# Attention units of a two-layer encoder: transposes and value products in pairs of steps, and the rounding of the outputs on GpSimd

## The reference

```
for l in range(DEPTH):                       # DEPTH = 2
    h = rmsnorm(x, norm_attn[l])
    z = h @ w_in[l]                          # columns are split among the groups
    o_a = gqa_axial_mixer(...)               # A: 8 heads of 64, softmax(q k^T) v
    o_b = mla_mixer(...)                     # B: 4 heads, scores of 96 channels
    o_c = diff_alibi_mixer(...)              # C: 4 heads, p1 - lambda p2
    x = x + concatenate([o_a, o_b, o_c]) @ w_out[l]
    h = rmsnorm(x, norm_ffn[l])
    x = x + conv_gated_mlp(h, ...)
return rmsnorm(x, final_norm)
```

## Time and profile before

| | us |
|---|---|
| median of 3 runs (2949.03 to 2953.87) | 2949.53 |
| the profiled execution, its own time | 2959.07 |
| its span, first to last instruction | 2957.3 |
| PE busy | 2864.6 |
| DVE busy | 1991.4 |
| ACT busy | 1315.0 |
| POOL busy | 460.7 |

### The profile page before, as it was taken

One profiled execution on the slowest core, in us unless ns is written; L12 is line 12 of the kernel. 1 busy time (PEld: TensorE's weight loads), 2 busy tenths in 40 slices (PEclk: granted clock), 3 DMA queues, 4 the chain that ended last, 5 costly groups with the idle time before them and its releaser, 6 DMA issues.

```text
span 2957.3 us, 36854 instructions
## 1 busy us (share of the span) xinstructions
PE 2864.6 (97%) x13552; PEld 2275.1 (77%) x13552; DVE 1991.4 (67%) x2316; ACT 1315.0 (44%) x1844; POOL 460.7 (16%) x243
## 2 busy tenths in 40 slices
PE   7999889999999999999999998899999999999998
PEld 6777646888888888888877785478788888888887
DVE  3987888982465565556678888889716555565555
ACT  4327888993322222222333288889724122222223
POOL 2111332233300000000131123322241000000002
PEclk9999999999999999999999999999999999999999
DMA  5455332431221111111135533244212111112102
GB/s 199 161 163 128 86 83 61 103 104 58 57 59 56 43 43 56 43 43 43 42 134 203 172 92 72 65 88 109 97 46 69 43 58 43 43 43 66 47 29 57
DMA packets 236532, 236.67 MB, mean 80 GB/s; under 512 B 59520, under 2 KB 199680, under 8 KB 236416
## 3 DMA queue, kind: packets, MB, share of 16 engines
q1 hardware_dynamic: 236416, 235.13, 28.1%
HBM read 184.24 MB, written 50.86 MB: 79 GB/s over the span
## 4 chain that ended last, share of the span: by engine, by line
PE 82%; DVE 10%; issue 4%; ACT 3%; DMA 1%; SPq 0%; ACTq 0%; POOL 0%; DVEq 0%
PE ps L1837 31%; PE ps L1852 16%; PE ps L1574 11%; PE ps L1676 9%; PE ps L1551 5%; PE ps L1714 4%; PE ps L1715 3%; DVE ps L1270 2%; PE ps L1817 1%; PE ps L1710 1%; DVE r L1255 1%; PE ps L1605 1%; DVE r L1298 0%; DVE r L1292 0%; DVE ch L1222 0%
## 5 line engine op out<-in xcount | busy, mean ns | idle before, releaser
L1676 PE MATMUL ps<-stack 128*128 128x512 f32 (+1 forms) x1152 | 350.5, 423 | 45.5 <-ACT prob L942 17.9
L1468 DVE TENSOR_TENSOR xT<-ps,xT 128x512 f32<-128x512 f32 x352 | 241.5, 691 | 209.8 <-PE ps L1852 209.5
L1676 PEld LDWEIGHTS ps<-stack 128*128 128x128 f32 (+1 forms) x1152 | 209.7, 194 | 160.1 <-ACT prob L942 51.5
L1551 PEld LDWEIGHTS ps<-ident_r,prob_r 128*128 128x128 f32 x2048 | 233.2, 143 | 101.3 <-issue 23.9
L942 ACT ACTIVATE prob<-ps,nmx 128x1024 f32<-128x1024 f32 x256 | 285.2, 1114 | 20.9 <-PE ps L1551 10.7
L1433 DVE SCALAR_TENSOR_TENSOR cv<-u,vec,cv 128x1024 f32<-128x1024 f32 x176 | 225.8, 1283 | 89.0 <-ACT cv L1083 78.7
L1378 DVE TENSOR_TENSOR ptl<-ps,pth 128x512 fp32r<-128x512 f32 x384 | 256.5, 685 | 38.6 <-ACT pth L1004 34.8
L1095 ACT ACTIVATE ah<-cv 128x1024 fp32r<-128x1024 f32 x44 | 46.7, 1061 | 528.9 <-DVE cv L1446 528.9
L1837 PE MATMUL ps<-xgh,w0h 128*128 128x512 f32 x704 | 274.7, 390 | 0.0
L1837 PE MATMUL ps<-xgl,w0h 128*128 128x512 f32 x704 | 273.9, 389 | 0.0
L1837 PE MATMUL ps<-xgh,w0l 128*128 128x512 f32 x704 | 273.9, 389 | 0.0
(11 more groups left out here) (245 smaller groups left out, 5555.6 us busy)
## 6 DMA issues: line engine op xcount, KB each, us to landing
wraw<-in_w_up SPq DMA_DIRECT2D x88, 512.0 KB, 5.0
draw<-in_w_down SPq DMA_DIRECT2D x22, 1024.0 KB, 4.9
stack<-ka_d SPq DMA_DIRECT2D x64, 256.0 KB, 5.6
wraw<-in_w_in SPq DMA_DIRECT2D x30, 512.0 KB, 4.2
vst<-v_d SPq DMA_DIRECT2D x48, 256.0 KB, 3.8
x_d<-xT SPq DMA_DIRECT2D x2, 4096.0 KB, 17.6
wraw<-in_w_out SPq DMA_DIRECT2D x16, 512.0 KB, 5.2
stack<-qc_d SPq DMA_DIRECT2D x64, 128.0 KB, 3.5
```

The source lines that it names most:

```text
L1468: ins = dve.tensor_tensor(xs, ps[:, 4 + j % 4, :], xs, ALU.add)
L1551: return pe.transpose(dst.bitcast(F32R), src, ident_r[:, :])
L1676: ins = pe.matmul(score_banks(i)[:, kh, :], st[q][0:rows, c0:c0 + P], st[k][0:rows, kh * HALF:(kh + 1) * HALF], start=n == 0, stop=n == le ...
```

## The change

A unit is **paired** when it is of A or B, three of its next unit's items are still to be made in it, and the unit after that is not of C. That holds for units 1 to 5 (B) and 16 to 30 (A) of each layer. In a paired unit:

- TensorE runs two steps at a time: a score item, the transposes of both steps, then the value products of both. The items come in steps 0, 2, 4 and 6 (they came in 1, 3, 5 and 7); the spread of the reciprocals comes in step 7 behind the products (it came in step 6).
- VectorE takes the maxima in steps 0, 2, 4 and 6, ahead of the low part.
- ScalarE makes the exponentials by a new table `PAIRED_EXP`: item 0 in step 0 ahead of the high copy, and items 1, 2 and 3 behind the high copies of steps 1, 3 and 5 (they came behind those of steps 0, 2, 4 and 6). `copy_norm` comes in step 7.

For all units of A and B, GpSimd writes the rounded result to `xgh` (a copy of 64 partitions x 512), between its own multiplication and its low part; ScalarE's `hi_mix` does nothing there any more. C is unchanged.

```diff
+        def paired(x, nx, after):
+            return x["group"] != "C" and own_items(nx) == 3 and not (after and after["group"] == "C")
+        PAIRED_EXP = {0: 0, 1: 1, 3: 2, 5: 3}
...
                 def lo_mix(x):
                     rows = slice(HD * x["par"], HD * x["par"] + HD)
+                    if x["group"] != "C":
+                        pool.tensor_copy(mix_at(xgh, x), osum[rows, :]).then_inc(mix_hi, 1)
                     pool.wait_ge(mix_hi, l * NU + x["u"] + 1)
...
                 def hi_mix(x):
+                    if x["group"] != "C":
+                        return
...
                 def act_unit(x, prev, nx, after):
                     for s in range(8):
                         second = nx and nx["group"] == "C"
-                        item = EXP_STEP_OF[own_items(nx)].get(s) if nx else None
-                        if second and item is not None:
+                        pairs = paired(x, nx, after)
+                        item = (PAIRED_EXP if pairs else EXP_STEP_OF[own_items(nx)]).get(s) if nx else None
+                        before_copy = second or pairs and s == 0
+                        if before_copy and item is not None:
                             exp_item(nx, item)
...
-                        if not second and item is not None:
+                        if not before_copy and item is not None:
                             exp_item(nx, item)
                         if s == 3 and prev:
                             copy_part(prev)
                         if s == 7 and prev:
                             hi_mix(prev)
-                        if s == (7 if x["group"] == "C" else 6):
+                        if s == (7 if x["group"] == "C" or pairs else 6):
                             copy_norm(x)
...
-                hi_mix(last)
...
+                        n = s + 1 if pairs else s
+                        if nx and n in STEP_OF[own_items(nx)]:
+                            max_item(nx, STEP_OF[own_items(nx)][n])
+                        if pairs:
+                            if s == 6 and after:
+                                max_item(after, 0)
...
+                        if pairs and s % 2 == 0:
+                            if s + 1 in STEP_OF[own_items(nx)]:
+                                score_item(nx, STEP_OF[own_items(nx)][s + 1])
+                            elif after:
+                                score_item(after, 0)
...
-                        if s >= LAG:
-                            value_product(x, s - LAG)
-                        elif prev:
-                            value_product(prev, 8 + s - LAG)
-                        if s == 6:
+                        if not pairs:
+                            products(s)
+                        elif s % 2:
+                            products(s - 1)
+                            products(s)
+                        if s == (7 if pairs else 6):
                             pe.wait_ge(dinv_done, l * NU + x["u"] + 1)
```

More of the change, by code:

```diff
@@ L1369, in dve_unit @@
                             mix_maps(nx, MIX_STEPS[s])
-                        if nx and s in STEP_OF[own_items(nx)]:
-                            max_item(nx, STEP_OF[own_items(nx)][s])
-                        if after and s in EARLY_STEP_OF[after["group"]]:
+                        pairs = paired(x, nx, after)
+                        n = s + 1 if pairs else s
[4 more added lines that the diff above has]
+                                max_item(after, 0)
+                        elif after and s in EARLY_STEP_OF[after["group"]]:
                             max_item(after, EARLY_STEP_OF[after["group"]][s])
@@ L1732, in pe_unit, with products @@
                 def pe_unit(x, prev, nx, after):
-                    b = x["half"]
-                    for s in range(8):
-                        if nx and s in STEP_OF[own_items(nx)]:
+                    b, pairs = x["half"], paired(x, nx, after)
+                    def products(n):
+                        if n >= LAG:
+                            value_product(x, n - LAG)
+                        elif prev:
+                            value_product(prev, 8 + n - LAG)
+                    for s in range(8):
+                        if pairs and s % 2 == 0:
[3 more added lines that the diff above has]
+                                score_item(after, 0)
+                        elif not pairs and nx and s in STEP_OF[own_items(nx)]:
                             score_item(nx, STEP_OF[own_items(nx)][s])
-                        if after and s in EARLY_STEP_OF[after["group"]]:
+                        if after and not pairs and s in EARLY_STEP_OF[after["group"]]:
                             score_item(after, EARLY_STEP_OF[after["group"]][s])
```

## The result

The changed kernel takes 2999.75 us (median of 4 runs, 2996.58 to 3005.87) against 2950.95 us before (4 runs): ratio 1.0162, 95% interval 1.0148 to 1.0176. Forecast were 2988.0 us, 2956 to 3010, slower with 0.88. Its profiled execution took 2998.46 us.

What follows compares the result with a forecast made beforehand. PE, busy 97%, was taken as the bound, with VectorE and ScalarE nearly full in A. Per layer 15 x 1.15 + 5 x 0.4 = 19.3 us, 38.5 for two, on the median 2949.53 gave 2988.0 us, range 2956 to 3010.

Steps and rivals of the forecast that it cites:

- The signs: Profile marks listed beforehand: longer periods, VectorE idle ahead of `sum_output`, PE idle ahead of step 6's transposes, PE below 92% in A.
- PE's own work: Per pair, transposes lose 0.05 us and the second value product gains 0.07: net gain 0.02, 3 us over 40 paired units.
- The new wait in A: Per paired unit, late `copy_part` holds VectorE, then PE at steps 6 and 7: 1.40 us, net +1.15 on 10.89.
- 1.6 if all small waits stay: Upper end given for the +1.15 us per paired unit of A; it entered the range's top as 30 x 1.6.
- B, 0.4 us: Per paired unit of B, the same chain with longer items: PE waits 0.50 us, less 0.08, so +0.4 us.
- I cost the relief at nothing: ScalarE losing 24 rounding copies of 0.626 us per layer: nothing gained, at most 0.4 us per unit of A.
- GpSimd's copy: The 64 x 512 rounding copy on GpSimd: taken as 1.29 us, hidden behind GpSimd's idle time.
- The first: Rival: the wait never forms if `copy_part` is done at about 2.4 us; 15 us faster, 2934 us; chance 0.09.
- the main case: The full wait forms in paired units, `copy_part` ending at 3.24 us after step 3's start: 2974 to 3004 us, chance 0.68.
- The second, half the wait: Rival: step 6 stalls but VectorE recovers, or `copy_part` starts sooner; +0.2 to +0.8 us per A unit, 2956 to 2974; chance 0.12.
- The third, a falling clock: Rival: PE's clock falls as well, one to four falls worth 5 us each over both layers, 2993 to 3008 us; chance 0.08.

Runs made afterwards that it cites:

- e3: The changed kernel with `copy_part` directly behind the high copy of step 3, ahead of the exponential, in paired units: 2969.59 us, ratio 1.0054 to the kernel before.
- e4: The changed kernel with `sum_output` two steps later (step 5 instead of 3) in paired units: 2962.45 us, ratio 1.0028 to the kernel before.
- e8: No unit paired, GpSimd rounds, `copy_part` in step 4 behind the exponential in units of A and B: 3043.42 us, ratio 1.0306 to the kernel before.
- e7: e4 with the value product lagging two steps instead of three, in every unit: 2947.52 us, ratio 0.9982 to the kernel before.
- e9: The changed kernel with no unit paired, GpSimd still rounding, value product lagging two steps instead of three: 2946.09 us, ratio 0.9980 to the kernel before.
- e2: The changed kernel with the rounding back on ScalarE for every unit, so the pairs alone: 3013.64 us, ratio 1.0204 to the kernel before.

## Why the prediction was right

It was right in direction, range and mechanism. The median lies 11.8 us above the number, and by the periods the difference can be placed: 8 us in A, 3 in B, and 1 in the median of the kernel before, which stood that much higher here. The signs came as listed: VectorE idle 1.0 us ahead of `sum_output` (0.7 to 1.0 forecast), PE idle 1.24 us ahead of step 6's transposes (1.1), PE 90% busy in A (below 92%), and no wait of GpSimd for ScalarE in A's units. e3 and e4 took the wait away in two ways and most of the loss went with it; e8 made it without pairs.

- **PE's own work, 0.02 us saved per pair.** Right in its parts, not confirmed as a gain. In the timeline above eight transposes take 571.95 - 571.32 = 0.63 us, and a product behind a product starts after 0.23 (572.25 to 572.48 in the same timeline). But only 24 of the 49 runs of eight in 500 to 650 us take 0.63 to 0.65; 11 take 0.71 to 0.75 and 14 take 0.97 or more, since the low parts come late. e7 against e9 measures nothing for it. The 81 ns per transpose of the Trainium skill ("TensorE: Matmul & The Clock Gate", Back-to-back issue gap), by which pairing would have won 11 us, did not show in the time either: e9 is not slower than e7.
- **The new wait in A, 1.40 us.** Right in every link, short by 0.3 in size. Zero, the start of step 3's transposes, is 569.40 - 0.34 = 569.06. High copy at 1.14 (forecast 1.07), exponential 1.63 (1.56), `copy_part` 2.85 (2.65), `sum_output` 3.48 (3.27), maximum 4.20 (3.99), low part 5.46 (5.12), transposes 6.20 (5.87), due at 4.81 (4.79). The wait was 1.39, not 1.08. The step that was mis-sized is the two distances taken from instructions in another neighbourhood: exponential to `copy_part` is 1.22, not 1.09, and maximum to low part 1.26, not 1.13 (in every other head it is 1.14, see below). What follows was right: in the unit before, the run of eight behind the wait took 0.97 us (562.88 to 563.85) instead of 0.63, 0.34 more, where I had 0.08 + 0.24. With 1.41 per unit instead of 1.15 the term is 30 x 0.26 = 8 us short. It also lies above the upper end that the prediction's own terms give: "1.6 if all small waits stay" does not come out of them, since 11.8 + 0.4 - 10.89 is 1.3. With 1.3 the term ends at about 2993 us. So it is partly luck that the range holds the result: it reached higher by that slip and by room for a clock that did not fall.
- **B, 0.4 us.** Measured 0.70, short by 3 us in all, for the same links.
- **"I cost the relief at nothing".** Wrong as a statement: e2 gives it 12 us inside the change. It did not hurt the sum, because the chain was worked out without a rounding copy at the head of a paired unit, so that what this copy would have cost was not counted either.
- **GpSimd's copy.** It took 0.61 us (0.60 in the row below), half of what I took and near ScalarE's 0.63; hidden, as said. The 0.77 us of the Trainium skill ("GPSIMD Engine Reference", Elementwise) was nearer than my row.
- **The rivals.** The first was decided where it was placed: `copy_part` was done at 3.44 after step 3's start, where the rival needed 2.4 and the main case had 3.24. The second, half the wait, did not come: each unit of A lost 1.41 us. The third, a falling clock, did not come in the change (granted clock 1.00 in 500 to 650 us), but did in e8.

The row of GpSimd's copy, from the changed kernel's timeline:

```profile
562.45 0.60 POOL L722 CAST xgh<-osum 64x512 f32 x1 [0.17 <-POOL osum L716]
```

## What to carry to other kernels

When three engines are each over 95% busy and meet through in-order lists, follow one unit of work through every list before regrouping one of them; the change lost some 32 of 49 us to one exponential that had slipped ahead of a copy another engine was waiting for. Put the instruction that another engine needs ahead of the long one that nobody is waiting for yet, and when work is grouped in pairs, check that slots are freed a whole pair earlier. Do not count on a saving on one full engine while the next engine is as full: the pairing, freed of its two waits, measured as no gain.

## What the runs showed of the hardware that was not expected

**The half of the partitions costs 0.12 us.** In the changed kernel the low part starts 1.26 us after the maximum that follows `sum_output` for two units, and 1.14 us for the next two, in turn through A; the period alternates 12.38 and 12.24 with it. The two kinds, from the changed kernel's timeline:

```profile
548.63 1.23 DVE L1284 TENSOR_REDUCE nmx<-ps 128x1 f32<-128x1024 f32 x1
549.77 1.28 DVE L1394 TENSOR_TENSOR ptl<-ps,pth 128x512 fp32r<-128x512 f32 x2
```

against 573.26 and 574.52 above. Two units are one head, and heads alternate between the lower and upper 64 partitions in `sum_output`. The Trainium skill ("VectorE: DVE Perf Modes", Two Vector instructions with no wait between them) gives as a model that an instruction is held until all earlier ones have finished when its input starts in another quadrant (32 partitions) than the last input from that memory. The trace agrees: the low part is the first to read SBUF after `sum_output`, and where it is held it starts 0.03 us after the maximum's end (574.49) instead of 0.09 us before it. On ScalarE `copy_part`, which reads 64 partitions behind an exponential over 128, starts 1.22 us after it where a high copy starts after 1.09. No run here separates the cause on ScalarE.

**The clock fell in e8 and not in the changed kernel.** The two have nearly the same PE busy time in 500 to 650 us (134.32 and 134.75 us), but e8 was granted 0.91 and the changed kernel 1.00. Part of e8's busy time is work at half speed: it holds 757 matmuls against 827. The wait of PE in each unit is longer in e8 (1.54 us against 1.24). Whether that decides was not tried.
